# Output projection of a hybrid decoder step: tokens in rows in place of features in rows

## The chip, the cores and the metric

The kernel runs on one core of a Trainium2 chip. The metric is the device time of one execution in microseconds (us), taken as the median over several runs. The engines are TensorE (PE for its matmuls, PEld for its weight loads), VectorE (DVE), ScalarE (ACT), GpSimd (POOL) and SyncE (SP, which here issues the loads of weights). TensorE's clock has two levels, 1.2 and 2.4 GHz; the profile gives the granted clock of a stretch as a share of the full one (0.50 or 1.00 where it does not change within the stretch).

## The reference

One inference step of a decoder with two layers, over 264 tokens: 256 of a prompt and 8 of a sample group, all in float32, with a model width of 1024. Cut to what matters here:

```python
for i in range(DEPTH):                       # DEPTH = 2
    h = rms_norm(x, P['norm_mix_g'][i])
    ...                                      # layer 0: RWKV-7, layer 1: GLA
    mixed = jnp.concatenate([tok, mem_attention(q_mem, mem_k[i], mem_v[i])], axis=-1)
    x = x + mixed @ P['w_out'][i]            # output projection, 1024 x 1024
    x = x + hier_moe(rms_norm(x, P['norm_ffn_g'][i]), P['router_wg'][i], P['router_bg'][i],
                     P['router_we'][i], P['router_be'][i], P['exp_w_up'][i], P['exp_w_down'][i])
```

`hier_moe` takes the logits of 4 groups and 32 experts (36 columns, 40 with padding), picks a group and two experts in it for each token, and runs them as SwiGLU networks with weights of 1024 x 1024 and 512 x 1024 for each of 32 experts.

## The kernel before, in words

The engines' programs are written out by hand, and semaphores join them. Tokens lie in three row blocks, `TILES`: 128 and 128 rows of the prompt and 8 rows of the sample. `x` holds the residual with tokens in rows, `mixedT` the mixers' output with its 1024 features in rows (8 blocks of 128, `KT = 8`) and the 264 tokens as columns. `ps` are the eight PSUM banks.

The output projection of layer l is `output(l)` of TensorE's program. Before the change it makes the result with features in rows. Two halves of `w_out` (512 columns each, `chunk_in()` or `wo1`) give four groups each, so n runs from 0 to 7. Group n is eight matmuls of 128x264 (L775: the weights loaded into the array are a 128x128 block of `w_out`, and `mixedT` moves), then three products by `ident` that add x, turned, into the same bank (L778). ScalarE copies the bank to `oT` (L1314). While the next group runs, `finish(n - 1)` takes `oT` for the router's logits (L759, three products of 40 columns, raw, since the norm's scale comes later) and turns it back to tokens in rows (L763, three transposes). VectorE copies these to x (L1817, L1818) and ScalarE takes their squares (L1561) for the norm. `finish(7)` ends the projection. Behind it stand 41 products of `ident` that nothing reads (`idle_products(WARM[0])`, L749).

VectorE's `route(l)` then adds up the squares (L1654), makes the norm's scale, scales the logits (L1659), and picks the groups and experts until `gates` (L1682). TensorE's next piece, the tokens' ranks in their experts (L1190), waits for `gates`. Then come a few more idle products, the gather of the tokens for the first experts (L1100), and the expert units (L1119), whose weights SyncE loads into a ring of 8 buffers (`load_unit`, L380). A load beyond the ring's eighth waits until TensorE has used a buffer (`m_used`). At the start of `output(l)` TensorE waits for `t_dve` (VectorE's last piece of `mixedT`) and for `router_s` (VectorE has scaled the router's weights `wr` and cleared `ss8`, L1813).

Of the kernel before, what the change touches and what calls it, by code (L numbers as in the profile page):

```python
# [6 lines left out]
ALU = mybir.AluOpType  # L7
# [11 lines left out]
TS = 8  # L19
# [22 lines left out]
EPS = 1e-6  # L42
GN_EPS = 64e-5
# [10 lines left out]
def tiles_through(g):  # L54

    total = 0
    for i, m in enumerate([2, 2] + [w // 128 for _, w in W_IN0[1:]] + [4, 4]):
        total += LORA_TILES.get(i, 0) + m
        if i == g:
            return total  # L60


CHUNKS = 3 + len(W_IN0)
# [91 lines left out]
shift_in shiftT_ps xj lora_s t_dve t_act sum_ps c_ps c_dve c_act c_zero oT_ps o_x dec_out gla_in  # L155
kv1w_in kv1_ps kv1_out kT1_ps kv1_stored vec2_in vec2 k1_in gnorm_in w1_in0 w1_in1 w1_in2 w1_in3 kT1_in p1_ps p1_out
# [4 lines left out]
def build(nc, A, O, dbg=None):  # L161
    with ExitStack() as ctx:
# [199 lines left out]

        oT = [arena[:, AR + 128 + T * n:AR + 128 + T * (n + 1)] for n in range(2)]
# [19 lines left out]
        def _(sp):  # L383
# [66 lines left out]
            def mixer1():  # L450
                sp.dma_start(gng, A["gla_norm_g"][0:1, :].broadcast_to([128, 192])).then_inc(s["gnorm_in"], 16)
                sp.wait_ge(s["kv1_stored"], 48)
                sp.dma_start(kT_1, kT_scr.rearrange("p (a b) -> p a b", a=2)).then_inc(s["kT1_in"], 16)
# [48 lines left out]
            for l in range(DEPTH):  # L502
# [3 lines left out]
                for n in range(UNITS * NQ):  # L506
# [3 lines left out]
                    if n in (6, 7):  # L510
                        sp.wait_ge(s["pj_ps"], tiles_through(n + 2) + 8 * l)
# [104 lines left out]
        def _(pe):  # L616
            sel = lambda b, n: ident[0:TS, b:b + 1].broadcast_to([TS, n])

            def transpose_h(n):
                pe.wait_ge(s["norm_h"], 6 * n - 3)  # L620
                pe.wait_ge(s["pj_out"], tn[0])
# [129 lines left out]
            def output(l):  # L751

                def finish(n):

                    pe.wait_ge(s["pj_out"], tn[0] - (0 if n == KT - 1 else 1))
                    if KT * l + n >= 2:
                        pe.wait_ge(s["o_x"], KT * l + n - 1)
# [9 lines left out]
                n = 0  # L767
                for half in range(2):
                    buf = chunk_in() if l == 0 else wo1[half]
                    if l == 1:  # L770
                        pe.wait_ge(*((s["w1_in0"], 48) if half else (s["w1_in3"], 32)))
                    for b in range(4):
                        p = bank()
                        for i in range(KT):
                            pe.matmul(p[:, 0:T], buf[:, 512 * i + 128 * b:512 * i + 128 * (b + 1)], mixedT[:, i, :], start=(i == 0), stop=False)  # L775

                        for t, (c, m) in enumerate(TILES):
                            last = pe.matmul(p[:, c:c + m], x[0:m, t, 128 * n:128 * (n + 1)], ident[0:m, 0:m], start=False, stop=(t == 2))  # L778
                        tile_done(last)
                        if n > 0:  # L780
                            finish(n - 1)
                        n += 1
                finish(KT - 1)
                idle_products(WARM[0])

# [135 lines left out]
            def mixer1():  # L921
# [33 lines left out]
                pe.wait_ge(s["kT1_in"], 16)  # L955
# [294 lines left out]
        def _(act):  # L1250
# [298 lines left out]
            for l in range(DEPTH):  # L1549
# [7 lines left out]
                def squares(n):  # L1557

                    act.wait_ge(s["o_x"], KT * l + n + 1)
                    for t, (_, m) in enumerate(TILES):  # L1560
                        last = act.activation(h[0:m, t, 128 * n:128 * (n + 1)], x[0:m, t, 128 * n:128 * (n + 1)], ACT.Square, accum_out=ss8[0:m, t, n:n + 1])  # L1561
                    last.then_inc(s["o_sq"], 1)

                for n in range(KT):
                    if n >= 2:
                        act.wait_ge(s["oT_ps"], KT * l + n - 1)
                    out(oT[n % 2], 128)
                    if n == 1:
                        act.wait_ge(s["router_s"], l + 1)
                    if n > 0:  # L1570
                        squares(n - 1)
                squares(KT - 1)
# [41 lines left out]
        def _(dve):  # L1614
# [37 lines left out]
            def route(l):  # L1652
                dve.wait_ge(s["o_sq"], KT * (l + 1))
# [3 lines left out]
                dve.wait_ge(s["logit_ps"], l + 1)  # L1657
# [80 lines left out]
            def setup():  # L1738
# [69 lines left out]
            def output(l):  # L1808
# [5 lines left out]
                for n in range(KT):  # L1814
                    dve.wait_ge(s["oT_ps"], KT * l + n + 1)
                    cols = slice(128 * n, 128 * (n + 1))
                    dve.tensor_copy(x[:, 0:2, cols], ps[2 + n % 2][:, 0:256].rearrange("p (t d) -> p t d", t=2))  # L1817
                    mark(dve.tensor_copy(x[0:TS, 2, cols], ps[2 + n % 2][0:TS, 256:384]), "o_x", KT * l + n + 1)  # L1818
# [178 lines left out]
            def mixer1():  # L1997
# [62 lines left out]
                dve.wait_ge(s["gnorm_in"], 16)  # L2060
# [107 lines left out]
```

## Time and profile before

| what | value |
|---|---|
| median of 3 runs | 1671.73 us (1666.05 to 1673.22) |
| the profiled execution's own time | 1672.15 us |
| its span in the trace | 1670.2 us |
| granted TensorE clock, mean over the span | 0.872 |
| PE busy | 1282.9 us (77%) |
| DVE, ACT, POOL busy | 25%, 15%, 1% of the span |
| read from HBM | 455.12 MB, 277 GB/s over the span |

The busy shares are means over stages with different limits, so none of them says what the stage around the projection is worth. The time outside the span is 1.95 us. The profiled execution is 0.42 us above the median.

### The profile page before, as it was taken

The numbers are of one execution on the slowest core, as the hardware profiler recorded it, in microseconds if no ns is written. First come the engines' busy times: TensorE is split into PE (matmuls) and PEld (weight loads), VectorE is DVE, ScalarE is ACT, GpSimd is POOL, SyncE is SP. The second block draws the span as 40 slices with busy tenths as digits, with TensorE's granted clock in tenths as the row PEclk, the third lists the DMA queues.
The fourth block names the chain that finished last, engine by engine and source line by source line (L and its number), as shares of the span: only waits on it lengthen the run. The fifth ranks groups of instructions, "written<-read, shape, count | busy, mean of one in ns | idle before, by whom it ended". The sixth has DMA issues, their size and how long they took to land.

```text
span 1670.2 us, 21379 instructions
## 1 busy us (share of the span) xinstructions
PE 1282.9 (77%) x9492; PEld 702.9 (42%) x9492; DVE 412.9 (25%) x828; ACT 249.4 (15%) x656; POOL 18.0 (1%) x53
## 2 busy tenths in 40 slices
PE   2968996879977685967665999879977666967754
PEld 1556786877633231513211665548613213312311
DVE  4044567841311011011012132521211011011002
ACT  2110331241201000001001322312201000100100
POOL 1000000000000000000000000000000000000000
PEclk9958899899989778799898887779989987889886
DMA  9410201038499999999997813428599999999993
GB/s 304 148 47 26 76 5 44 18 132 352 161 409 409 409 409 409 408 409 409 409 410 291 268 48 57 163 76 317 236 408 409 408 409 408 409 409 409 409 409 154
DMA packets 147475, 463.65 MB, mean 278 GB/s; under 512 B 12858, under 2 KB 37212, under 8 KB 147180
## 3 DMA queue, kind: packets, MB, share of 16 engines
q1 hardware_dynamic: 145980, 457.78, 71.2%
q0 software_dynamic: 1392, 4.38, 0.8%
q8 instruction: 78, 1.28, 0.3%
q14 instruction: 25, 0.20, 0.0%
HBM read 455.12 MB, written 7.02 MB: 277 GB/s over the span
## 4 chain that ended last, share of the span: by engine, by line
PE 47%; DMA 38%; DVE 7%; SPq 3%; issue 2%; ACT 2%; DVEq 0%; ACTq 0%
DMA slot<-in_exp_w_up 26%; PE bank L1119 8%; PE bank L656 6%; DMA arena<-in_exp_w_up 6%; DMA slot<-in_exp_w_down 6%; PE bank L1100 5%; PE bank L775 4%; PE bank L887 4%; SPq L380 3%; PE bank L940 3%; PE bank L934 3%; PE bank L1130 2%; PE bank L749 1%; PE bank L742 1%; PE bank L675 1%
## 5 line engine op out<-in xcount | busy, mean ns | idle before, releaser
L1119 PE MATMUL bank<-slot,hT 128*32 128x512 f32 x1536 | 232.0, 723 | 133.8 <-DMA slot<-in_exp_w_up 133.8
L1119 PEld LDWEIGHTS bank<-slot,hT 128*32 128x32 f32 x1536 | 49.5, 123 | 301.6 <-DMA slot<-in_exp_w_up 175.9
L1719 DVE SCALAR_TENSOR_TENSOR mixedT<-mixedT,bank 128x512 f32<-128x512 f32 x16 | 11.0, 688 | 509.8 <-ACT mixedT L1275 509.8
L1119 PE MATMUL bank<-slot,mixedT 128*32 128x512 f32 x768 | 100.9, 669 | 37.4 <-DMA slot<-in_exp_w_down 30.6
L1119 PE MATMUL bank<-arena,hT 128*32 128x512 f32 x512 | 80.2, 707 | 40.8 <-DMA arena<-in_exp_w_up 40.8
L1130 PE MATMUL bank<-mixedT,arena 128*128 128x512 f32 (+1 forms) x192 | 90.2, 612 | 12.8 <-ACT mixedT L1284 12.8
L1100 PE MATMUL bank<-arena,h 128*128 128x128 f32 (+1 forms) x384 | 81.8, 351 | 12.1 <-DVE arena L1712 7.8
L1275 ACT ACTIVATE mixedT<-bank 128x512 f32<-128x512 f32 x16 | 9.6, 597 | 532.8 <-PE bank L1119 532.8
L1100 PEld LDWEIGHTS bank<-arena,h 128*128 128x128 f32 (+1 forms) x384 | 62.6, 222 | 37.3 <-issue 12.6
L1731 DVE TENSOR_TENSOR x<-bank,x 128x512 f32<-128x512 f32 (+1 forms) x96 | 66.0, 687 | 36.2 <-PE bank L1130 36.2
L1100 PE MATMUL bank<-gain,h 128*128 128x128 f32 (+1 forms) x384 | 74.8, 329 | 0.0
L775 PE MATMUL bank<-mixedT,slot 128*128 128x264 f32 x256 | 64.3, 407 | 9.7 <-issue 9.7
L1119 PEld LDWEIGHTS bank<-slot,mixedT 128*32 128x32 f32 x768 | 24.0, 119 | 110.6 <-issue 51.1
L1100 PEld LDWEIGHTS bank<-gain,h 128*128 128x128 f32 (+1 forms) x384 | 57.1, 204 | 25.0 <-issue 12.3
L1725 DVE COPY mixedT<-bank 128x512 f32<-128x512 f32 x16 | 11.1, 692 | 225.8 <-PE bank L1119 225.8
L656 PE MATMUL bank<-slot 128*128 128x264 f32 x288 | 64.8, 386 | 0.6 <-ACT arena L1314 0.6
L1130 PEld LDWEIGHTS bank<-mixedT,arena 128*128 128x128 f32 (+1 forms) x192 | 28.4, 161 | 75.9 <-issue 75.9
L1270 ACT ACTIVATE hT<-bank,gainT 128x128 f32<-128x128 f32 x128 | 36.6, 368 | 156.7 <-PE bank L1100 156.7
L656 PEld LDWEIGHTS bank<-slot 128*128 128x128 f32 x288 | 54.6, 190 | 10.3 <-ACT arena L1314 1.0
L775 PEld LDWEIGHTS bank<-mixedT,slot 128*128 128x128 f32 x256 | 50.4, 202 | 18.8 <-DVE arena L1995 8.0
L1119 PEld LDWEIGHTS bank<-arena,hT 128*32 128x32 f32 x512 | 17.5, 120 | 93.4 <-issue 48.7
L1119 PE MATMUL bank<-arena,mixedT 128*32 128x512 f32 x256 | 39.3, 744 | 13.0 <-DMA arena<-in_exp_w_down 6.7
(448 smaller groups left out, 1497.1 us busy)
## 6 DMA issues: line engine op xcount, KB each, us to landing
slot<-in_exp_w_up SPq DMA_DIRECT2D x96, 2048.0 KB, 24.1
slot<-in_exp_w_down SPq DMA_DIRECT2D x48, 2048.0 KB, 24.0
arena<-in_exp_w_up SPq DMA_DIRECT2D x32, 2048.0 KB, 23.6
arena<-in_exp_w_down SPq DMA_DIRECT2D x16, 2048.0 KB, 23.6
slot<-in_w_in SPq DMA_DIRECT2D x6, 1536.0 KB, 7.1
slot<-in_w_out SPq DMA_DIRECT2D x4, 2048.0 KB, 8.6
slot<-in_w_in SPq DMA_DIRECT2D x3, 2048.0 KB, 8.0
slot<-in_w_in SPq DMA_DIRECT2D x5, 1024.0 KB, 5.6
```

The source lines that it names most:

```text
L380: sp.dma_start(ring[buf], src.rearrange("e p n -> p e n")).then_inc(sem, 16)
L656: last = pe.matmul(p[0:m, 0:n], w(k), rhs(k), start=(k == 0), stop=(k == kt - 1))
L675: last = pe.matmul(ps[4 + m][:, :], mem[:, m, 128 * k:128 * (k + 1)], w[:, k, :], start=(k == 0), stop=(k == KT - 1))
L775: pe.matmul(p[:, 0:T], buf[:, 512 * i + 128 * b:512 * i + 128 * (b + 1)], mixedT[:, i, :], start=(i == 0), stop=False)
L887: last = pe.matmul(out, lt(c)[rows, q, :], rh(c)[rows, q, :], start=(i == 0), stop=(i == len(MM[name]) - 1))
L934: last = pe.matmul(p[0:m, 0:T], w(k)[:, c0:c0 + m], rhs(k), start=(k == 0), stop=(k == kt - 1))
L940: last = pe.matmul(p[:, 0:384], hT[:, k, 128 * t:128 * (t + 1)], w[:, k, :], start=(k == 0), stop=(k == KT - 1))
L1100: last = pe.matmul(ps[bank][:, 128 * (k % 4):128 * (k % 4 + 1)], h[0:m, t, 128 * k:128 * (k + 1)], G[par][0:m, t, :], start=(t == 0), stop ...
L1119: last = pe.matmul(ps[bank + half][rows, :], lhs[:, rows], ring[buf][:, e, half * FF:(half + 1) * FF], start=first, stop=last_)
L1130: return pe.matmul(ps[SC_BANK[o]][0:m, :], ST[:, c:c + m], yq[:, FF * n:FF * (n + 1)], start=True, stop=True)
L1270: last = act.activation(xs[par][:, k, :], ps[bank][:, 128 * (k % 4):128 * (k % 4 + 1)], ACT.Copy, scale=gainT[:, KT * l + k:KT * l + k + 1])
L1731: return dve.tensor_tensor(xt, ps[SC_BANK[o]][0:m, :], xt, ALU.add)
```

## The change

The projection is made with tokens in rows. The matmuls of a half now have 128 tokens of `mixedT` as weights, and 512 columns of `w_out` move (`tokens`). The eight sample rows are made by products that have the last 32 columns of `mixedT` as weights, the i-th in column group i % 4 of the array, so that a bank holds four partial sums (`samples`). ScalarE copies that bank to `oS`, and a product with the new constant `pick` adds the four up (`samples_sum`). VectorE adds the banks to x (`add_tokens`, `add_samples`); the three products that added x in TensorE are gone. When x is there, it is turned once, by feature block, for the logits (`transposes`, `logits`), with ScalarE's copy to `oT` between. ScalarE's squares are six of up to 512 columns for a layer in place of 24 of 128. The wait for `router_s` stands ahead of the transposes, no more at the projection's start. `pick` is built by one VectorE operation at the program's start, and two small loads now share a semaphore (`gnorm_in`).

```diff
-                def finish(n):
...
-                    for t, (c, m) in enumerate(TILES):
-                        last = pe.matmul(ps[4 + t][0:m, 0:LG], oT[n % 2][:, c:c + m], wr[:, n, :], start=(n == 0), stop=(n == KT - 1))
...
-                    for t, (c, m) in enumerate(TILES):
-                        last = pe.transpose(ps[2 + n % 2][0:m, 128 * t:128 * (t + 1)], oT[n % 2][:, c:c + m], ident[:, :])
-                    last.then_inc(s["oT_ps"], 1)
+                def tokens(half, t):
+
+                    p = ps[2 * half + t]
+                    for i in range(KT):
+                        last = pe.matmul(p[:, :], mixedT[:, i, 128 * t:128 * (t + 1)], buf[:, i, :], start=(i == 0), stop=(i == KT - 1))
+                    tile_done(last)
+
+                def samples(half):
+
+                    for i in range(KT):
+                        last = pe.matmul(ps[4 + half][32 * (i % 4):32 * (i % 4 + 1), :], mixedT[:, i, T - 32:T], buf[:, i, :], start=(i < 4), stop=(i >= 4))
+                    tile_done(last)
+
+                def samples_sum(half):
+
+                    pe.wait_ge(s["o_sb"], O_STEPS * l + half + 1)
...
+                    pe.matmul(ps[7][0:TS, :], pick[:, :], oS[half], start=True, stop=True).then_inc(s["o_ps"], 1)
+
+                def transposes(n):
+
+                    if n >= 2:
+                        pe.wait_ge(s["o_sb"], O_STEPS * l + n + 1)
+                    for t, (c, m) in enumerate(TILES):
+                        last = pe.transpose(ps[n % 2][:, c:c + m], x[0:m, t, 128 * n:128 * (n + 1)], ident[0:m, 0:m])
+                    last.then_inc(s["o_ps"], 1)
+
+                def logits(n):
+
+                    pe.wait_ge(s["o_sb"], O_STEPS * l + n + 3)
                     for t, (c, m) in enumerate(TILES):
                         last = pe.matmul(ps[4 + t][0:m, 0:LG], oT[n % 2][:, c:c + m], wr[:, n, :], start=(n == 0), stop=(n == KT - 1))
-                    if n == KT - 1:
-                        last.then_inc(s["logit_ps"], 1)
...
-                pe.wait_ge(s["router_s"], l + 1)
...
-                    for b in range(4):
-                        p = bank()
-                        for i in range(KT):
-                            pe.matmul(p[:, 0:T], buf[:, 512 * i + 128 * b:512 * i + 128 * (b + 1)], mixedT[:, i, :], start=(i == 0), stop=False)
...
+                    tokens(half, 0)
+                    if half == 0:
+                        tokens(half, 1)
+                        samples(half)
+                samples(1)
+                samples_sum(0)
+                tokens(1, 1)
+                samples_sum(1)
+                pe.wait_ge(s["router_s"], l + 1)
+                pe.wait_ge(s["o_x"], 6 * l + 4)
+                for n in range(KT):
+                    if n == 4:
+                        pe.wait_ge(s["o_x"], 6 * (l + 1))
+                    transposes(n)
+                    if n > 0:
+                        logits(n - 1)
+                logits(KT - 1)
                 idle_products(WARM[0])
...
+                link(dve.tensor_reduce(pick[:, :], ident[:, :].rearrange("p (j n) -> p n j", j=4)[:, 32 - TS:32, :], AXX, ALU.add))
...
+                def add_tokens(half, t, tile):
...
+                    dve.tensor_tensor(x[:, t, cols], ps[2 * half + t][:, :], x[:, t, cols], ALU.add).then_inc(s["o_x"], 1)
```

On TensorE, this is the start of the projection and the end of its first group before the change (the names behind the arrow are what is read, the first before it what is written):

```order
L775 MATMUL bank<-mixedT,slot 128x264 [waits chunk_in2,pj_out,router_s,t_dve]
L775 MATMUL bank<-mixedT,slot 128x264 x7
L778 MATMUL bank<-ident,x 128x128 x2
L778 MATMUL bank<-ident,x 128x8
L775 MATMUL bank<-mixedT,slot 128x264 [waits pj_out]
```

After the change the same place reads:

```order
L762 MATMUL bank<-slot,mixedT 128x512 [waits chunk_in2,t_dve]
L762 MATMUL bank<-slot,mixedT 128x512 x15
L768 MATMUL bank<-slot,mixedT 32x512 x8
L762 MATMUL bank<-slot,mixedT 128x512 [waits chunk_in0]
L762 MATMUL bank<-slot,mixedT 128x512 x7
```

The 128x264 matmuls with their three adding products have become 128x512 matmuls and 32x512 ones, and the wait for `router_s` has left this place.

Before the change each group's `finish` stands between the wide matmuls of the groups, on TensorE as:

```order
L759 MATMUL bank<-wr,arena 128x40 [waits pj_out]
L759 MATMUL bank<-wr,arena 128x40
L759 MATMUL bank<-wr,arena 8x40
L763 MATMUL bank<-ident,arena 128x128 x2
L763 MATMUL bank<-ident,arena 8x128
```

After the change these rows repeat, eight of them behind all wide matmuls and right ahead of the 41 idle products (a step of the tail):

```order
L783 MATMUL bank<-ident,x 128x128 [waits o_sb]
L783 MATMUL bank<-ident,x 128x128
L783 MATMUL bank<-ident,x 128x8
L790 MATMUL bank<-wr,arena 128x40 [waits o_sb]
L790 MATMUL bank<-wr,arena 128x40
L790 MATMUL bank<-wr,arena 8x40
```

The logits and the transposes have moved from between the wide matmuls to one run without any wide matmul in it, and the transposes now read x, not `oT`.

## Rows read from the trace of the kernel before

**Rows 1.** Windows around both projections: us, busy (x count) of each engine, PEclk, DMA share, GB/s.
```profile
379.10:383.00 3.90, 3.82 (x9) 3.03 (x10) 0.00 (x0) 0.00 (x0) 0.00 (x0) 0.50 0.94 320
383.00:425.30 42.30, 42.30 (x240) 36.16 (x239) 4.27 (x14) 9.04 (x44) 0.00 (x0) 1.00 0.82 322
...
425.30:446.70 21.40, 21.40 (x172) 18.03 (x174) 11.39 (x64) 7.71 (x24) 0.00 (x0) 1.00 0.24 92
446.70:900.00 453.30, 329.04 (x1972) 121.68 (x1968) 51.32 (x77) 31.24 (x87) 0.00 (x0) 0.86 1.02 407
1118.80:1123.70 4.90, 4.83 (x11) 3.83 (x12) 0.00 (x0) 0.00 (x0) 0.00 (x0) 0.50 0.98 329
```

**Rows 2.** Timeline, TensorE's weight loads: start, us, line, operation, xcount [idle before <-releaser].
```profile
379.15 5.32 PEld L775 LDWEIGHTS bank<-mixedT,slot 128*128 128x128 f32 x16 [7.98 <-DVE arena L1995]
...
423.29 0.67 PEld L759 LDWEIGHTS bank<-wr,arena 128*128 128x128 f32 x6
...
424.03 0.26 PEld L763 LDWEIGHTS bank<-ident,arena 128*128 128x128 f32 x3
...
424.31 0.67 PEld L759 LDWEIGHTS bank<-wr,arena 128*128 128x128 f32 x6
...
425.33 9.23 PEld L749 LDWEIGHTS bank<-ident 128*128 128x128 f32 x82
...
1118.84 0.29 PEld L775 LDWEIGHTS bank<-mixedT,slot 128*128 128x128 f32 x1 [1.95 <-DVE arena L2079]
...
1165.52 0.41 PEld L749 LDWEIGHTS bank<-ident 128*128 128x128 f32 x3
```

**Rows 3.** Chain of waits: start, us, engine, line, xcount of a link.
```profile
54.11 13.75 PE bank L675 x32
...
436.56 8.24 PE bank L1100 x48
...
444.81 13.91 PE bank L1119 x128
...
575.95 14.99 PE bank L1100 x48
```

**Rows 4.** Timeline, VectorE ahead of layer 0's projection.
```profile
378.09 0.06 DVE L1995 MEMSET arena<- 128x1 f32 x1
...
379.00 0.08 DVE L1813 MEMSET arena<- 128x24 f32 x1
```

**Rows 5.** Timeline, VectorE's routing and TensorE's wait for it, layer 0.
```profile
430.23 0.58 DVE L1659 SCALAR_TENSOR_TENSOR arena<-bank,arena,br 128x40 f32<-128x40 f32 x3
...
434.59 0.18 PE L1190 MATMUL bank<-arena,before_h 128*128 128x32 bf16 x1
```

**Rows 6.** Windows elsewhere, for the granted clock.
```profile
69.00:73.20 4.20, 4.14 (x26) 2.55 (x24) 0.00 (x0) 3.08 (x8) 2.02 (x3) 1.00 0.38 130
...
371.40:376.20 4.80, 0.00 (x0) 0.00 (x0) 1.23 (x2) 3.37 (x4) 0.00 (x0) 1.00 0.03 6
...
575.95:590.90 14.95, 14.95 (x49) 11.36 (x49) 1.38 (x2) 1.74 (x5) 0.00 (x0) 0.50 1.03 411
...
955.10:959.90 4.80, 3.68 (x23) 2.50 (x22) 0.86 (x2) 4.24 (x11) 0.00 (x0) 1.00 0.76 208
960.00:976.90 16.90, 16.90 (x47) 10.71 (x47) 6.76 (x9) 2.52 (x4) 0.00 (x0) 0.50 0.09 32
...
1112.00:1117.20 5.20, 4.98 (x18) 2.78 (x18) 0.00 (x0) 2.08 (x6) 0.00 (x0) 0.50 0.00 0
```

**Rows 7.** Timeline, three transposes of row blocks (128, 128, 8 rows), twice.
```profile
72.08 0.37 PEld L626 LDWEIGHTS bank<-ident,h 8*128 8x128 f32 x3 [0.17 <-issue]
...
1113.43 0.49 PEld L1092 LDWEIGHTS bank<-ident,slot 8*128 8x128 f32 x3 [0.33 <-issue]
```

**Rows 8.** Page, costliest groups: line, operation, xcount, busy us, mean ns, idle before.
```profile
L1275 ACT ACTIVATE mixedT<-bank 128x512 f32<-128x512 f32 x16 | 9.6, 597 | 532.8 <-PE bank L1119 532.8
...
L1731 DVE TENSOR_TENSOR x<-bank,x 128x512 f32<-128x512 f32 (+1 forms) x96 | 66.0, 687 | 36.2 <-PE bank L1130 36.2
```

More of the change, by code:

```diff
@@ L56, in tiles_through @@
     total = 0
-    for i, m in enumerate([2, 2] + [w // 128 for _, w in W_IN0[1:]] + [4, 4]):
+    for i, m in enumerate([2, 2] + [w // 128 for _, w in W_IN0[1:]] + [3, 3]):
         total += LORA_TILES.get(i, 0) + m
@@ L154 @@
 cache_k cache_v qn_ps qn qb_ps s_score sT_ps s_max s_exp s_prob spT_ps spT sat_ps sat_out
-shift_in shiftT_ps xj lora_s t_dve t_act sum_ps c_ps c_dve c_act c_zero oT_ps o_x dec_out gla_in
-kv1w_in kv1_ps kv1_out kT1_ps kv1_stored vec2_in vec2 k1_in gnorm_in w1_in0 w1_in1 w1_in2 w1_in3 kT1_in p1_ps p1_out
+shift_in shiftT_ps xj lora_s t_dve t_act sum_ps c_ps c_dve c_act c_zero o_ps o_sb o_x dec_out gla_in
+kv1w_in kv1_ps kv1_out kT1_ps kv1_stored vec2_in vec2 k1_in gnorm_in w1_in0 w1_in1 w1_in2 w1_in3 p1_ps p1_out
 g_abs g_log g_dec g_sub g_exp g_mul kh_ps kh_out ga_ps ga_out gd_ps gz go_ps go_out gsq gs_a gs_vps gs_add gs_q gs_ps gs_out g_tanh g_silu gm_ps
@@ L361, in build @@
         assert b_.at <= 12288, b_.at
+        oS = [arena[:, 3400 + 512 * n:3400 + 512 * (n + 1)] for n in range(2)]
+        pick = sb("pick", TS)
         oT = [arena[:, AR + 128 + T * n:AR + 128 + T * (n + 1)] for n in range(2)]
@@ L767, in output @@
-                n = 0
+                    last.then_inc(s["logit_ps"], 1)
                 for half in range(2):
-                    buf = chunk_in() if l == 0 else wo1[half]
+                    buf = k3((chunk_in() if l == 0 else wo1[half])[:, 0:KT * 512], KT)
                     if l == 1:
                         pe.wait_ge(*((s["w1_in0"], 48) if half else (s["w1_in3"], 32)))
-                    for b in range(4):
-                        p = bank()
-                        for i in range(KT):
-                            pe.matmul(p[:, 0:T], buf[:, 512 * i + 128 * b:512 * i + 128 * (b + 1)], mixedT[:, i, :], start=(i == 0), stop=False)
-                        for t, (c, m) in enumerate(TILES):
[L778 to L782, printed above, removed]
@@ L1555, in _, with squares, copy_samples @@
                     mixer1()
[L1557 to L1562, printed above, removed]
+                def squares(half, t, at):
+                    m = TILES[t][1]
+                    act.wait_ge(s["o_x"], 6 * l + at)
+                    cols = slice(512 * half, 512 * (half + 1))
+                    act.activation(h[0:m, t, cols], x[0:m, t, cols], ACT.Square, accum_out=ss8[0:m, t, half:half + 1]).then_inc(s["o_sq"], 1)
+                def copy_samples(half):
+                    act.wait_ge(s["pj_ps"], tn[0] + 6 * l + (3, 5)[half])
+                    act.copy(oS[half], ps[4 + half][:, :]).then_inc(s["o_sb"], 1)
+                copy_samples(0)
+                act.wait_ge(s["router_s"], l + 1)
+                squares(0, 0, 1)
+                squares(0, 1, 2)
+                copy_samples(1)
+                squares(1, 0, 3)
+                squares(0, 2, 4)
                 for n in range(KT):
+                    act.wait_ge(s["o_ps"], O_STEPS * l + n + 3)
                     if n >= 2:
[L1566 to L1572, printed above, removed]
+                        act.wait_ge(s["logit_ps"], KT * l + n - 1)
+                    act.copy(oT[n % 2], ps[n % 2][:, 0:T]).then_inc(s["o_sb"], 1)
+                    if n < 2:
+                        squares(1, n + 1, 5 + n)
                 act.wait_ge(s["rs"], l + 1)
@@ L1813, in output, with add_samples @@
                 dve.memset(ss8, 0.0).then_inc(s["router_s"], 1)
[L1814 to L1818, printed above, removed]
+                def add_tokens(half, t, tile):
+                    cols = slice(512 * half, 512 * (half + 1))
+                    dve.wait_ge(s["pj_ps"], PROJECTED + 6 * l + tile)
+                    dve.tensor_tensor(x[:, t, cols], ps[2 * half + t][:, :], x[:, t, cols], ALU.add).then_inc(s["o_x"], 1)
+                def add_samples(half):
+                    cols = slice(512 * half, 512 * (half + 1))
+                    dve.wait_ge(s["o_ps"], O_STEPS * l + half + 1)
+                    dve.tensor_tensor(x[0:TS, 2, cols], ps[7][0:TS, :], x[0:TS, 2, cols], ALU.add).then_inc(s["o_x"], 1)
+                add_tokens(0, 0, 1)
+                add_tokens(0, 1, 2)
+                add_tokens(1, 0, 4)
+                add_samples(0)
+                add_tokens(1, 1, 6)
+                add_samples(1)
+                dve.wait_ge(s["o_x"], 6 * (l + 1))
                 mark(dve.memset(sq[:, 0:1], 0.0), "x_out", l + 1)
```

22 lines of the change are left out of this document (11 added, 11 removed).

## The prediction

> **What bounds the kernel now.** I read the windows around the projections first. From 446.7 us the DMA engines are full (share 1.02, 407 GB/s), and they stay so to 900; ahead of that, from 425.3 to 446.7, they are nearly idle (0.24) while TensorE is busy for all of 21.40 us [rows 1]. The ring's eight buffers are loaded by then, and the next load waits for the first expert unit to release one. So the experts' stream of weights sets the end, and TensorE's run from the start of the projection to the first released buffer sets when that stream begins. A microsecond taken from this run moves the stream and the end by a microsecond; this holds once for each layer.
>
> Second, the timeline of TensorE. In layer 0 the projection begins at 379.15 and its last group hands over to the idle products at 425.33, which is 46.18 us; in layer 1 it is 1118.84 to 1165.52, 46.68 us; together 92.86 [rows 2]. TensorE is busy in all of it but 0.1 us [rows 1], so there is no stall to win, only work. The clock is at 0.50 (1.2 GHz) for the first 3.9 us of layer 0's projection and the first 4.9 us of layer 1's [rows 1]: what is done there takes twice as long.
>
> Third, what stands behind: TensorE's ranks (L1190) begin at 434.59, right behind the idle products, which take about 9.3 us from 425.33 [rows 2, 5]. VectorE's routing, which they also wait for, runs from 430.23 until then, 4.36 us from the scaled logits to the gates [rows 5].
>
> **The new work at full clock, a layer.** Token tiles: 32 matmuls of 128x512. The nearest row is 16 such matmuls (32 records, two for each float32 matmul) in 13.75 us, 0.859 each [rows 3], so 27.50. Samples: 16 products of 32x512 in four column groups, shaped like the experts' first products, 64 of which take 13.91 us (128 records) [rows 3], 0.217 each, so 3.48. Two sums of the partials are 512-column products without company: 1.72. Then the tail, eight steps of three transposes and three 40-column products. Transposes of row blocks cost 0.37 and a gap of 0.17 [rows 7]; logits 0.74, from 423.29 to 424.03 [rows 2]; a step is 1.28 and the tail 10.24. The sum is 27.50 + 3.48 + 1.72 + 10.24 = 42.94, for both layers 85.88.
>
> **The start.** TensorE no longer waits for `router_s` there, so it follows the VectorE memset that ends at 378.15, not the one that ends at 379.08 [rows 4]: 0.93 us earlier in layer 0; I take 0.95 for each layer, 1.9 together. The slow stretch stays. If the clock rises at the same moments as before, it is 4.85 and 5.85 us long and half of it is lost: 2.4 + 2.9 = 5.3 us. (If it rises as long after the start as before, 4.4.)
>
> **Hidden parts.** VectorE's adds of 0.69 us [rows 8] lie beside matmuls: the tail's first transpose needs the half 0 columns, added while tile (1, 1) runs for 6.9 us, and step 4 needs the last adds, some 1.5 us of work, behind 5.1 us of tail. Were they late, the price is those 1.5 us. ScalarE's 512-column squares (0.60 [rows 8], with their accumulators perhaps 0.8) stand between the copies to `oT`; a step of 1.28 covers a copy and two steps a square, and without that cover two squares would cost 1 to 1.5 us a layer. The squares are done before the logits, so the norm's scale leaves the path behind them; but the gates would then be ready 4.4 us after the logits while the idle products take 9.3, so this earns nothing, and hides up to 4.9 us of delay on VectorE. `pick` adds one small reduction to VectorE's start: its nearest is a product of 128x40 in 0.19 (three in 0.58 [rows 5]), so +0.2 us at most, and below nothing isn't possible. The merged semaphore waits for two loads issued one behind the other: 0.
>
> With the clock at full in the tail the change is worth 92.86 − (85.88 + 5.3 − 1.9) = 3.6 us, less 0.2: 3.4. This is 1668.8 against the profiled execution's 1672.15, which lies 0.42 above the median, and 1668.3 on the median's scale, on which all that follows stands.
>
> **The clock in the tail.** Before, thin work stood between wide matmuls, and the clock stayed at 1.00 from 383.0 to 446.7 [rows 1]. Now 10 us hold nothing but transposes and 40-column products. The trace has such stretches. At 69.0 to 73.2 TensorE ran 24 transposes, 4.14 us busy, at 1.00 [rows 6]. From 955.1 to 959.9, 4.80 us of mainly transposes and thin products (3.68 busy), were granted 1.00, and 960.0 begins a stretch at 0.50 [rows 6]; likewise 371.4 to 376.2, idle, ahead of the slow start at 379.1 [rows 1, 6]. So rows of thin work stand on both sides, one that kept the clock and two (one without any work) that ended in a fall; the tail is twice as long as any of them.
>
> The Trainium skill ("TensorE: Matmul & The Clock Gate", Part 4: PE-mode transpose) says the full clock doesn't engage for transpose mode, which "doesn't count as PE-busy the same way". That speaks against this change; the 4.2 us of transposes at 1.00 disagree over that length, the fall at 960 agrees. By the page alone the whole tail would be slow, the slower rival below.
>
> The price: I place the fall as far into the tail as the two stretches that ended in one are long, 4.8 us; 5.44 us are left, 4.25 steps. At 0.50 three transposes take 0.49 + 0.33 = 0.82 in place of 0.54 [rows 6, 7]. For the logits the bounds are 0.74 (all overhead) and 1.48 (all clock); the transposes' ratio is 1.52, that of the gather 14.99/8.24 = 1.82 [rows 3, 6]; between them I take 1.24, nearer the gather, which is matmuls too. A step is then 2.06, 0.78 more; 4.25 steps give 3.3. The idle products then begin slow and need, as at the starts, 3.9 to 4.9 us to raise the clock [rows 1], half of which is lost: 2.2. So 5.5 a layer, 11.0 for both: 11.0 − 3.4 = 7.6 above before, **1679.3**.
>
> Ends: with the fall 2.2 us in (half of the transposes' 4.2 us) it is 6.3 steps, +7.1 a layer, 1682.5; 7.5 us in, 2.1 steps, +3.9, 1676.1; logits at 1.48 add up to 1.0 a layer, 1.02 for 0.78 a step. The own range of this case is 1675 to 1684.
>
> **Rivals.**
> *The clock holds in the tail* (1668.3). For it: the transposes at 69.0 to 73.2. Against it: the fall at 960 and the tail's length.
> *It falls in one layer only*, half of the 11.0: 1673.8. For it: the two layers' clocks do not rise equally long after the start [rows 1].
> *The clock falls at the tail's very start* in both layers: eight steps, 6.2, and 2.2 are +8.4 a layer, 16.8 − 3.4 = 13.4 above before, 1685.1. It decides the sign of my test once the loss is over 5.9 us a layer (8.4 + 3.4, halved). Against it: 4.2 us of transposes at full clock.
> *Faster than before:* the clock holds and the tail is cheaper than priced, since transposes behind other work took 0.28 (424.03 to 424.31) and logits 0.67 [rows 2], a step of 0.95: 16 × 0.33 = 5.3 less, 1663.0. It passes 0.5% from 0.31 a step on. Against it: the 0.28 are transposes that read a full-height `oT`; the gap of 0.17 stood where row blocks of 8 were turned [rows 7], as here.
> That the projection isn't the path can't be: the DMA engines wait for it [rows 1].
>
> **How the numbers follow.** A measurement of this kernel can tell about 0.5%, 8.4 us, from no change; so faster is below 1663.4 and slower above 1680.1. Chances: the fall part way into the tail in both layers 0.55, the clock holds 0.22, one layer 0.08, the early fall 0.08, the cheap tail 0.07. The first case's own range reaches from 1675 to 1684, with somewhat under half of it above 1680.1, say 0.24 of the 0.55; with the early fall, slower is 0.32. Faster is the cheap tail, 0.07. The rest, 0.61, is the same. The range takes in all but the cheap tail: from 1666.5, which is the held clock less the 0.9 for an earlier rise at the start and less half a microsecond of execution spread (0.42, the profiled one above the median), rounded, to the early fall with the layers' rounding, 1685.5.
>
> **What would show it.** Right: eight steps of the tail on TensorE behind the sum of the samples, steps of about 1.3 us and then of about 2.1, a granted clock of 0.50 in the end of the tail and the start of the idle products in both layers; token tiles of 6.9 us, samples of 1.7; TensorE's gather at 1.00; L1190 begins behind idle products with the gates ready before. Wrong: a clock of 1.00 through the tail, TensorE's sample products at 0.8 us each (no company in the column groups, 16 × 0.64 = 10 us a layer more), waits for `o_sb` or `o_x` between the steps, or a stream that begins at a time other than the first released buffer.

## The result, and the profile after

The changed kernel takes 1674.27 us (1670.86 to 1676.86, 13 runs) against 1667.63 us of the kernel before (1663.66 to 1674.63, 13 runs). The ratio is 1.0034 with an interval of 1.002 to 1.0049: 5.7 us slower, between 3.3 and 8.2. The forecast was 7.6 us above the kernel before.

The first view is TensorE's timeline of layer 0 in the changed kernel, which answers to [rows 2]: start, duration, line, operation, count of records.

```profile
377.51 15.95 PE L762 MATMUL bank<-slot,mixedT 128*128 128x512 f32 x32 [6.84 <-DVE arena L2050]
393.39 1.93 PE L768 MATMUL bank<-slot,mixedT 128*32 128x512 f32 x16
395.25 7.13 PE L762 MATMUL bank<-slot,mixedT 128*128 128x512 f32 x16
402.31 1.92 PE L768 MATMUL bank<-slot,mixedT 128*32 128x512 f32 x16
404.05 1.02 PE L776 MATMUL bank<-arena,pick 128*8 128x512 f32 x2
...
413.02 1.11 PE L783 MATMUL bank<-ident,x 128*128 128x128 f32 x6
414.09 0.81 PE L790 MATMUL bank<-wr,arena 128*128 128x40 f32 x6
...
417.87 0.81 PE L790 MATMUL bank<-wr,arena 128*128 128x40 f32 x6
418.61 0.63 PE L783 MATMUL bank<-ident,x 128*128 128x128 f32 x3
419.17 1.31 PE L790 MATMUL bank<-wr,arena 128*128 128x40 f32 x6
420.41 0.89 PE L783 MATMUL bank<-ident,x 128*128 128x128 f32 x3
...
423.29 2.55 PE L790 MATMUL bank<-wr,arena 128*128 128x40 f32 x12
425.77 11.07 PE L754 MATMUL bank<-ident 128*128 128x128 f32 x82
436.68 0.18 PE L1220 MATMUL bank<-arena,before_h 128*128 128x32 bf16 x1
```

The wide work of the changed kernel ends at 413.02, 12.3 us before the old projection's end at 425.33 [rows 2]. The tail spends this: the same logits take 0.74 us up to the step at 417.87 and 1.24 from 419.17 on (start to start), the transposes 0.53 and then 0.82. The tail ends at 425.77, and the 41 idle products take 10.9 us more, where they took 9.3 [rows 2, 5]. The ranks (L1220) start 2.1 us later than before in layer 0 [rows 5], although the projection began 1.64 us earlier.

The windows of the same kernel show why. They answer to [rows 1]; the number before the last two of each line is the granted clock.

```profile
377.50:381.40 3.90, 3.89 (x5) 1.81 (x6) 0.73 (x3) 0.00 (x0) 0.00 (x0) 0.50 0.69 229
...
413.00:418.90 5.90, 5.90 (x42) 4.34 (x41) 3.04 (x16) 2.94 (x9) 0.00 (x0) 1.00 1.02 409
418.90:425.80 6.90, 6.90 (x34) 5.27 (x32) 0.00 (x0) 3.16 (x6) 0.00 (x0) 0.51 0.18 71
...
1156.20:1159.80 3.60, 3.60 (x26) 2.59 (x25) 1.59 (x7) 2.18 (x7) 0.00 (x0) 0.99 0.99 361
1159.80:1170.50 10.70, 10.70 (x50) 8.04 (x49) 1.45 (x9) 3.90 (x8) 0.00 (x0) 0.50 0.29 114
1170.50:1173.90 3.40, 3.40 (x19) 3.40 (x19) 3.02 (x25) 1.11 (x2) 0.00 (x0) 0.58 0.00 0
```

TensorE is busy in every microsecond of the tail, so no wait for ScalarE's copies is at work. The clock falls from 1.00 to 0.50 inside the tail, 5.9 us into it in layer 0 and 3.6 us in layer 1, and the idle products behind it begin at the low level (0.58 over the last window). In the changed kernel VectorE has the gates long before TensorE reads them:

```profile
429.96 0.26 DVE L1722 TENSOR_TENSOR arena<-arena 128x96 bf16<-128x96 f32 x1
```

That operation ends at 430.22, and the ranks that wait for it start at 436.68: 6.46 us of idle products stand between. In the kernel before, the same operation ends at 434.50, and the ranks start at 434.59 [rows 5]:

```profile
434.24 0.26 DVE L1682 TENSOR_TENSOR arena<-arena 128x96 bf16<-128x96 f32 x1
```

SyncE's first load that waits for a released buffer shows what the end of the kernel sees of all this. In the kernel before it stands at 446.7 [rows 1] and, in layer 1, with the program's last matmuls below it, so:

```profile
1186.91 3.80 SPq L380 DMA_DIRECT2D slot<-in_exp_w_down  x3
...
1643.51 3.64 PE L1119 MATMUL bank<-slot,mixedT 128*32 128x512 f32 x16 [1.89 <-DMA slot<-in_exp_w_down]
1647.94 7.89 PE L1130 MATMUL bank<-mixedT,arena 128*128 128x512 f32 x12 [0.80 <-ACT mixedT L1284]
```

In the changed kernel:

```profile
448.81 3.80 SPq L385 DMA_DIRECT2D slot<-in_exp_w_down  x3
...
1193.23 3.80 SPq L385 DMA_DIRECT2D slot<-in_exp_w_down  x3
...
1649.98 1.92 PE L1149 MATMUL bank<-slot,mixedT 128*32 128x512 f32 x16 [1.69 <-DMA slot<-in_exp_w_down]
1652.70 5.48 PE L1160 MATMUL bank<-mixedT,arena 128*128 128x512 f32 x12 [0.80 <-ACT mixedT L1314]
```

The stream of layer 1 starts 6.3 us later and its last load lands 6.5 us later (the last unit starts at 1649.98, not 1643.51). The two profiled executions differ by 2.3 us only, since the last two pieces behind the stream took 1.92 and 5.48 us in one and 3.64 and 7.89 in the other: the granted clock over the last unit is 1.00 in the changed kernel's execution and 0.50 in the other's. These 4.1 us don't belong to the change: from the landing of the last load to the end of the span it is 26.7 us in the kernel before and 22.5 in the changed one, but 26.7 again in e9_weave_no_fill, which has the new projection too. A single execution scatters by that much, so below the length of the path is compared beside the ratios of many runs.

### The profile page after: what moved, and what is told of

It is laid out like the page before. It is cut to its first block, busy times and chain, and to the rows that moved or that the text cites. A ratio compares the mean times of both kernels' runs of the same rounds, so it can differ in the third digit from the quotient of the medians.

```text
span 1672.5 us, 20962 instructions
## 1 busy us (share of the span) xinstructions
PE 1306.3 (78%) x9340; PEld 679.6 (41%) x9340; DVE 411.4 (25%) x809; ACT 242.5 (15%) x588; POOL 18.0 (1%) x53
## 4 chain that ended last, share of the span: by engine, by line
PE 49%; DMA 36%; DVE 7%; SPq 3%; issue 3%; ACT 2%; DVEq 0%; ACTq 0%
DMA slot<-in_exp_w_up 25%; PE bank L1149 9%; PE bank L661 6%; DMA arena<-in_exp_w_up 6%; DMA slot<-in_exp_w_down 6%; PE bank L1130 5%; PE bank L762 4%; PE bank L917 4%; PE bank L970 3%; PE bank L964 3%; SPq L385 3%; PE bank L1160 2%; PE bank L754 1%; PE bank L790 1%; PE bank L747 1%
## 5 line engine op out<-in xcount | busy, mean ns | idle before, releaser
L1149 PE MATMUL bank<-slot,hT 128*32 128x512 f32 x1536 | 242.0, 752 | 127.9 <-DMA slot<-in_exp_w_up 127.8
L1149 PE MATMUL bank<-arena,hT 128*32 128x512 f32 x512 | 84.6, 737 | 34.7 <-DMA arena<-in_exp_w_up 34.7
L1130 PE MATMUL bank<-arena,h 128*128 128x128 f32 (+1 forms) x384 | 88.2, 371 | 15.5 <-DVE arena L1752 15.5
L1130 PEld LDWEIGHTS bank<-arena,h 128*128 128x128 f32 (+1 forms) x384 | 67.4, 238 | 43.0 <-DVE arena L1752 17.3
L1130 PE MATMUL bank<-gain,h 128*128 128x128 f32 (+1 forms) x384 | 68.4, 309 | 0.0
L762 PE MATMUL bank<-slot,mixedT 128*128 128x512 f32 x128 | 61.4, 638 | 7.8 <-DVE arena L2050 6.8
L1130 PEld LDWEIGHTS bank<-gain,h 128*128 128x128 f32 (+1 forms) x384 | 52.5, 189 | 23.4 <-issue 9.0
L970 PE MATMUL bank<-slot,hT 128*128 128x384 f32 x128 | 47.5, 532 | 0.0
```

The lines of the kernel that those rows point to most:

```text
L762: last = pe.matmul(p[:, :], mixedT[:, i, 128 * t:128 * (t + 1)], buf[:, i, :], start=(i == 0), stop=(i == KT - 1))
L970: last = pe.matmul(p[:, 0:384], hT[:, k, 128 * t:128 * (t + 1)], w[:, k, :], start=(k == 0), stop=(k == KT - 1))
L1130: last = pe.matmul(ps[bank][:, 128 * (k % 4):128 * (k % 4 + 1)], h[0:m, t, 128 * k:128 * (k + 1)], G[par][0:m, t, :], start=(t == 0), stop ...
L1149: last = pe.matmul(ps[bank + half][rows, :], lhs[:, rows], ring[buf][:, e, half * FF:(half + 1) * FF], start=first, stop=last_)
```

## The experiments

For each kernel the table gives the path: from the end of VectorE's small memset ahead of the projection, which the changed projection follows within 0.05 us, to the first product of the ranks, layer 0 plus layer 1, from the timelines. The ratio is that of runs against the kernel before on the same chip.

| kernel | path, us | against before | ratio (95% interval) |
|---|---|---|---|
| before | 56.44 + 56.94 = 113.38 | | 1 |
| changed | 59.22 + 61.42 = 120.64 | +7.26 | 1.0034 (1.002 to 1.0049) |
| e1_idle22 | 54.97 + 57.17 = 112.14 | −1.24 | 0.9999 (0.9982 to 1.0015) |
| e2_spread | 55.67 + 56.07 = 111.74 | −1.64 | 0.9995 (0.9975 to 1.0015) |
| e3_turn_by_matmul | 65.72 + 66.74 = 132.46 | +19.08 | 1.0077 (1.0057 to 1.0098) |
| e4_samples_twice | 63.09 + 64.87 = 127.96 | +14.58 | 1.0068 (1.0047 to 1.0089) |
| e5_weave | 52.57 + 53.60 = 106.17 | −7.21 | 0.9939 (0.9927 to 0.9952) |
| e6_before_idle31 | 56.40 + 56.90 = 113.30 | −0.08 | 1.0006 (0.9992 to 1.002) |
| e7_before_start | 55.98 + 56.50 = 112.48 | −0.90 | 1.0000 (0.9987 to 1.0014) |
| e8_spread_idle19 | 54.10 + 54.98 = 109.08 | −4.30 | 0.9992 (0.9981 to 1.0004) |
| e9_weave_no_fill | 53.70 + 53.26 = 106.96 | −6.42 | 0.9955 (0.9938 to 0.9973) |
| e10_spread1 | 55.17 + 56.19 = 111.36 | −2.02 | 0.9988 (0.9976 to 1.0) |
| e11_weave_fill1 | 52.18 + 52.58 = 104.76 | −8.62 | 0.9960 (0.9945 to 0.9975) |
| e12_turn_fill1 | 58.23 + 59.34 = 117.57 | +4.19 | one run, 1671.39 us |

Behind the path nearly everything is as long in one kernel as in another. From the first product of the ranks to SyncE's first load that waits for a released buffer it is 12.13 or 12.14 us in all fourteen profiles and both layers, but for one (layer 1 of e6_before_idle31, below); from that load to the landing of the layer's last one it is 456.4 to 457.6 us. So the stream of weights hides nothing of the path. The ratios follow the paths only roughly all the same: e3_turn_by_matmul is 12.9 us slower (9.5 to 16.3) for a path longer by 19.1, e8_spread_idle19 1.3 us faster (−0.7 to 3.2) for 4.3, and e5_weave 10.2 us faster (8.0 to 12.2) for 7.2. A path is that of one execution, and all that lies outside it adds up to between 1550.6 and 1558.4 us from one profile to the next. Why these three miss by more than their intervals stays open.

**Is it the clock?** The same 41 idle products, 16 of them moved into the tail (`FILL = 2`):

```diff
                     transposes(n)
                     if n > 0:
                         logits(n - 1)
+                    for _ in range(FILL):
+                        pe.matmul(ps[2][:, 0:128], ident[:, :], ident[:, :], start=True, stop=True)
                 logits(KT - 1)
-                idle_products(WARM[0])
+                idle_products(WARM[0] - FILL * KT)
```

> The changed kernel with the same 41 idle products, two of them after each of the tail's eight steps and 25 behind it. Theory (the clock falls because the tail holds thin work alone): the granted clock stays at 1.00 from the token tiles to the gather, steps are 1.26 + 0.45 = 1.71 us throughout, logits 0.74 in all of them, and the first released buffer comes 4.1 us earlier in layer 0 and 5.6 us in layer 1 than in the changed kernel; 9.7 in all, ratio about 0.9975. Rival (a step's length comes from the round trip over ScalarE's copy, and products put into it only fill a wait): no wide change of the steps, ratio 1.003. Rival (the clock falls from the tail however it is filled that lightly): steps grow to 2.06 + 0.9, ratio 1.003 to 1.006.

The windows over both tails of this kernel:

```profile
415.70:429.60 13.90, 13.90 (x105) 11.48 (x104) 3.04 (x16) 5.67 (x14) 0.00 (x0) 1.00 0.49 194
1152.50:1166.50 14.00, 14.00 (x105) 11.51 (x104) 3.04 (x16) 5.68 (x14) 0.00 (x0) 1.00 0.48 189
```

The clock stays at 1.00, steps are 1.75 us throughout with logits of 0.74, and the path is 8.9 us shorter than the changed kernel's with the same work in it: 9.7 were expected. The rival of a round trip over ScalarE falls: in a step that waits for a copy, products put in would fill the wait, but the steps grew by 0.49 us (from 1.26) for the 0.55 us of products put in. The ratio's interval doesn't exclude 0.9975, nor no difference to the kernel before, but it lies below the changed kernel's.

**One product a step** in place of two:

> The changed kernel with one idle product in each of the tail's steps (33 behind it), where e2_spread had two. If the theory is right that it is the share of wide work in the tail that decides, one product a step is the middle: either it holds (1.00 through the tail, from start to ranks 55.6 us as with two, ratio 0.9995) or the clock falls, later than in the changed kernel or as late, and the path is between 55.6 and 59.2 us in layer 0, ratio 1.001 to 1.003.

```profile
413.10:425.30 12.20, 12.20 (x89) 9.72 (x88) 3.05 (x16) 5.34 (x14) 0.00 (x0) 1.00 0.61 243
1148.00:1161.50 13.50, 13.50 (x92) 9.81 (x90) 3.74 (x17) 5.30 (x14) 0.00 (x0) 1.00 0.59 229
```

The clock stays at 1.00 in both layers, with 24 transposes in each tail, and the path is 55.2 us in layer 0 (55.6 expected).

**Is it the transposes?** The turning made by ordinary products, first in the changed kernel's order, then with one idle product a step:

```diff
-last = pe.transpose(ps[n % 2][:, c:c + m], x[0:m, t, 128 * n:128 * (n + 1)], ident[0:m, 0:m])
+last = pe.matmul(ps[n % 2][:, c:c + m], x[0:m, t, 128 * n:128 * (n + 1)], ident[0:m, 0:m], start=True, stop=True)
```

> The changed kernel with its 24 transposes a layer made as ordinary float32 products by the identity, everything else as it was. If it is the transposes that let the clock fall: the clock stays at 1.00 in the tail, a step costs perhaps 0.1 to 0.3 us more (1.4 to 1.55), and the 9.7 us come back less 1.6 to 4.8, ratio 0.998 to 1.0005. If the 40-column products alone are thin enough: the clock still falls 3 to 7 us into the tail, every step is longer by its slower turning, and the ratio is 1.005 to 1.008.

```profile
415.10:420.90 5.80, 5.80 (x41) 4.98 (x40) 2.97 (x16) 2.70 (x8) 0.00 (x0) 1.00 1.02 408
421.30:434.00 12.70, 12.70 (x54) 10.70 (x54) 0.00 (x0) 3.47 (x6) 0.00 (x0) 0.50 0.07 26
1161.70:1168.40 6.70, 6.70 (x48) 5.66 (x47) 3.04 (x16) 2.70 (x8) 0.00 (x0) 1.00 0.95 367
1168.80:1179.80 11.00, 11.00 (x48) 9.30 (x48) 0.00 (x0) 3.39 (x6) 0.00 (x0) 0.50 0.01 3
```

> The changed kernel with the turning made by ordinary products (as e3_turn_by_matmul) and one idle product in each step (as e10_spread1). If wide work of any kind keeps the clock and e3_turn_by_matmul was only a little short of it: 1.00 through the tail in both layers, steps of 1.93 us. If ordinary products in place of transposes are what lets it fall: 0.50 from some 4 to 7 us into the tail.

```profile
414.00:429.20 15.20, 15.20 (x113) 13.18 (x112) 3.04 (x16) 5.39 (x14) 0.00 (x0) 1.00 0.50 199
1153.60:1168.80 15.20, 15.20 (x113) 13.17 (x112) 3.04 (x16) 5.42 (x14) 0.00 (x0) 1.00 0.44 166
```

Without a single transpose the clock fell 6 to 7 us into the tail all the same, and with one more product in each step it stayed at 1.00. So the fall doesn't need transposes, and transposes don't force it: in these profiles, one of each kernel, the tails of either kind fell without the added product and held with it. Which part of a step lets the clock fall was not separated further; the 24 products of 40 columns are in every tail. The turning by ordinary products was dearer than the 0.1 to 0.3 us a step expected (steps of 1.70 us at full clock and 2.91 at half, against 1.26 and 2.06); the ratio, 1.0077, is among those expected for a fall (1.005 to 1.008).

**Does each microsecond count?** The sample products made twice:

```diff
-                    for i in range(KT):
+                    for i in [*range(KT), *range(KT)]:
```

> The changed kernel with the products of the sample rows made twice (the first pass's sums are overwritten by, or added to, the second's; the time alone is of interest). Theory (each microsecond of TensorE's work in the projection moves the end by one): 16 more products of 0.22 us a half, +1.8 us a half, +3.5 a layer, +7 in all, ratio 1.0076. Rival (the projection is partly hidden, as by loads of weights that are late anyway): under +2, ratio below 1.005.

```profile
406.84 3.64 PE L768 MATMUL bank<-slot,mixedT 128*32 128x512 f32 x32
```

These are the 16 products of half 1 in layer 0, 3.64 us in place of 1.92. The path is 7.3 us longer than the changed kernel's, as expected, and the ratio is 1.0068, 0.0034 (5.7 us) above it. With both intervals that is an estimated 1.4 to 10 us: the added work reaches the end, but the ratios alone don't tell whether all of it does.

**The slack in front of the gates.** The changed kernel with `WARM = (22, 5)`, then the kernel before with `WARM = (31, 5)`, then the spread tail with `idle_products(19)` behind it:

> The changed kernel with 22 idle products behind each projection in place of 41. Theory (TensorE's run up to the first released buffer sets the end, and the gates are ready some 4.4 us after the last logits, well ahead of the idle products' end at 10.9 us): the 19 products left out, 0.227 us each, come off the path in both layers, 4.3 us a layer, 8.6 in all, so from 1.0034 of the kernel before to about 0.998; the wait for the gates stays at 0 and the gather (L1130) stays at 8.4 us. Rival (the idle products also hold the clock up for the gather): the clock is at 0.50 when the gather begins, which then takes 15 us in place of 8.4, so about +2.3 a layer, ratio 1.006. Rival (the gates are late): TensorE waits for them as long as before, ratio 1.0034.

> The kernel before with 31 idle products in place of 41. Theory (before the change the routing ends together with the idle products, at 434.5, because the norm's scale comes after the last logits): TensorE waits for the gates for some 2.2 us in place of running products, the ranks begin at the same moment, ratio 1.000. Rival (the idle products alone held the ranks): 2.27 us a layer earlier, ratio 0.9973. If the clock falls in the wait, the gather takes 15 us in place of 8.2: ratio 1.008.

> The changed kernel with two idle products in each of the tail's steps and 19 behind it in place of 25. Theory (the gates come 4.4 us after the last logits, 19 products fill 4.3): 1.3 us a layer earlier than with 25, no wait for the gates over 0.3 us, the clock at 1.00 throughout; 2.6 us in all, ratio 0.998. Rival (the wait for the gates takes the place of the products): as with 25, 0.9995.

In the changed kernel the 19 products are pure waste: the path is 8.5 us shorter (8.6 expected), the gather keeps 8.41 us, and the ranks still start 2.2 and 1.9 us behind the gates. The ratio, 0.9999, is 0.0035 (5.8 us) below the changed kernel's; the 0.998 expected lies just outside its interval. In the kernel before, ten fewer leave the ranks where they were, since TensorE then waits; the first rank product in layer 0 of e6_before_idle31 reads

```profile
435.42 0.19 PE L1190 MATMUL bank<-arena,before_h 128*128 128x32 bf16 x1 [2.02 <-DVE arena L1682]
```

with 2.02 us of wait for the gates. That wait isn't always free. In layer 1 of the same run the clock was at 0.50 behind it, and the few idle products ahead of the gather took 2.50 us in place of 1.38:

```profile
1176.26 2.50 PE L749 MATMUL bank<-ident 128*128 128x128 f32 x10
1178.56 8.74 PE L1100 MATMUL bank<-arena,h 128*128 128x128 f32 x48
```

From the ranks to the first released buffer it was 13.60 us there, 1.47 more than elsewhere, which the path in the table does not show. In layer 0 the clock held.

So the early squares did take the norm off the routing (the gates come 4.4 us after the last step in the changed kernel, 9.2 in the kernel before), and this is worth nothing until idle products are taken out. With both, in the spread tail of e8_spread_idle19, the ranks start 0.06 us behind the gates, and the path is 2.7 us shorter than with 25 products; the ratio (0.9992; the 0.998 expected lies just outside its interval) doesn't separate the two.

**The start alone**, in the kernel before:

```diff
                 def finish(n):

+                    if n == 0:
+                        pe.wait_ge(s["router_s"], l + 1)
...
-                pe.wait_ge(s["router_s"], l + 1)
                 n = 0
```

> The kernel before with its wait for the router's weights (router_s) moved from the projection's start to the first logits: this part of the change alone. Theory: both projections start 0.95 us earlier and every later stage with them, 1.9 in all, ratio 0.9989. Rival (the start only moves the moment of the clock's rise, or the next wait takes its place): no gain, 1.000.

The projection follows the memset by 0.05 us in place of 1.0, but the path is shorter by 0.46 and 0.44 us only. The part of the projection at 0.50 is 4.9 and 5.9 us long, where it was 3.9 and 4.9 [rows 1]: the time won at the start is spent at half clock, and about half of it is lost. 0.9 us are below what the ratio can show.

**A version from these parts.** The sample products of both halves ahead of tile (1, 0), their sums among its matmuls, steps 0 to 3 between pairs of matmuls of tile (1, 1), steps 4 to 7 with idle products, 20 products behind (`WARM = (20, 5)`). VectorE's adds and ScalarE's squares are put in the matching order; cut to TensorE's part:

```diff
                 samples(1)
+                tokens(1, 0, 0, 2)
                 samples_sum(0)
-                tokens(1, 1)
+                tokens(1, 0, 2, 5)
                 samples_sum(1)
+                tokens(1, 0, 5, 8)
...
                     if n == 4:
+                        logits(3)
                         pe.wait_ge(s["o_x"], 6 * (l + 1))
                     transposes(n)
-                    if n > 0:
+                    if n > 0 and n != 4:
                         logits(n - 1)
+                    if n < 4:
+                        tokens(1, 1, 2 * n, 2 * n + 2)
+                    else:
+                        for _ in range(FILL):
+                            pe.matmul(ps[2][:, 0:128], ident[:, :], ident[:, :], start=True, stop=True)
```

with `FILL` 2, 0 and 1:

> The changed kernel in another order: both halves' sample products and their sums ahead of or among tile (1, 0), steps 0 to 3 of the tail between pairs of tile (1, 1)'s matmuls, steps 4 to 7 behind it with two idle products each, and 20 idle products at the end in place of 41. Theory (the new form of the projection is shorter work, the loss lies in the clock, and the idle products in excess of the routing's 4.4 us are waste): the clock stays at 1.00, and from the start of the projection to the ranks it is 1.9 + 33.6 + 8 x 1.26 + 1.8 + 4.5 = 51.9 us in layer 0 against 55.4 in the kernel before; with the earlier start some 4.4 us a layer, ratio about 0.9947. Rival (half of the tail without wide matmuls is still enough for the clock to fall): 0.50 in the last steps, 2 to 4 us a layer back, 0.998 to 1.000. Rival (the adds by VectorE are late for step 4): a wait of 1 us for o_x in each layer, 0.996.

> The woven order of e5_weave without the eight idle products in steps 4 to 7, whose thin run is then 5.1 us long. If the clock holds over it: 1.8 us a layer less than e5_weave, 3.6 in all, ratio about 0.992. If it falls there (in the changed kernel it fell 6.1 us into the tail in layer 0 and 3.6 us in layer 1): at least layer 1 loses, one or two steps of 0.8 us and idle products that begin at 0.50 (1.5 to 2 us): between 0 and 2 us of the 3.6 are left, ratio 0.993 to 0.995, with 0.50 shown in the end of the tail.

> The woven order with one idle product in steps 4 to 7 in place of two. As e10_spread1 kept 1.00 with one product in every step and e9_weave_no_fill fell without any, the clock should hold: 0.9 us a layer less than e5_weave, 1.8 in all, ratio 0.993 by the path (0.9928 from e5_weave's 0.9939), the gather at 8.4 us. If the clock falls in the last steps: 0.995 to 0.996 as e9_weave_no_fill.

With two products a step the path is 7.2 us shorter than the kernel before's (4.4 a layer expected, 3.9 and 3.3 came) and the ratio 0.9939 (0.9947 expected): faster than both kernels, as forecast. Step 4 does wait 0.24 us for VectorE's add:

```profile
420.90 0.59 PE L785 MATMUL bank<-ident,x 128*128 128x128 f32 x3 [0.24 <-DVE x L1876]
```

With none, the thin run of some 5 us ends in a fall in both layers; layer 1 shows it so:

```profile
1156.50:1161.50 5.00, 5.00 (x36) 3.77 (x36) 2.34 (x15) 2.54 (x7) 0.00 (x0) 0.98 0.94 332
1161.60:1164.50 2.90, 2.90 (x14) 2.90 (x14) 2.52 (x20) 2.61 (x3) 0.00 (x0) 0.50 0.33 134
```

and what the eight products left out a layer should save (3.6 us expected if the clock held) goes to slow idle products: the path is 0.8 us longer than with two. With one the clock holds and the path is the shortest, 1.4 us below that with two (1.8 expected), yet the ratio is 0.9960 against 0.9939, and the 0.9928 expected lies outside its interval. The two intervals overlap; which of the two is faster stays open.

## Why the prediction was right or wrong

The clock fell in the tail as forecast, and the time rose. The step of the prediction that failed is the one from the sum to the answer: "A measurement of this kernel can tell about 0.5%, 8.4 us, from no change". No row stood behind it; known were three runs of the kernel before, 7.2 us apart. On it a forecast of +7.6 us, 0.45%, went under "the same" with a chance of 0.61, and slower got 0.32. Thirteen runs of each kernel told 0.15%, and the +0.34% measured (0.20 to 0.49) stands clear of no change: slower. A forecast of 0.45% should have been read as slower.

In the sum itself three terms had the wrong size. The wide work was put at 65.4 us and took 67.5, the slow start at 5.3 and took 4.5, the slow idle products at 4.4 and took 3.0. That they leave the sum within 0.2 us of the measured path is luck, since the errors cancel.

The terms of the sum, both layers, against the changed kernel's timeline:

| term | forecast | measured |
|---|---|---|
| wide work at full clock | 65.4 | 67.5 (tiles 7.06, samples 1.74 to 1.86, sums 0.95) |
| the tail at full clock | 20.5 | 20.2 (steps of 1.26) |
| slow start, lost | 5.3 | 4.5 (15.88 and 16.82 for tiles of 14.12) |
| earlier start | −1.9 | −1.9 |
| the fall in the tail | 6.6 | 6.8 (2.6 and 4.2) |
| slow idle products | 4.4 | 3.0 (10.9 and 10.6 against 9.3) |
| path against before (92.9, start to idle products) | +7.4 | +7.3 |

- **The bound**, TensorE's run up to the first released buffer, stood: e4_samples_twice lengthened it by 7.3 us and the time with it, e2_spread and e1_idle22 shortened it, and the stream behind it was 456.4 to 457.6 us long in every profile. That a microsecond of it is a microsecond of time is not shown as exactly: three of the ratios in the table miss their paths by more than their intervals.
- **The prices** were good to a few hundredths where a row had the same shape: transposes at half clock were forecast at 0.82 and took 0.82, at full clock 0.54 and 0.53. Logits at half clock were forecast at 1.24 and took 1.24, but that was a choice between 0.74 and 1.48, so some luck is in it. The token tiles were taken from a row of 0.859 us a matmul and took 0.883; samples and sums were a little dearer too; together 2.1 us more.
- **The start**: the part at 0.50 was put at 4.85 and 5.85 us. In layer 0 the clock rose as long after the start as before, 3.9 us (window 377.50 to 381.40), which the prediction had named as the other case; in layer 1 the slow part was 5.9 us.
- **The fall** came in both layers, part way. It was placed at 4.8 us and came at 5.9 and 3.6, which nearly cancels: luck again. The rivals that the clock holds, that it falls in one layer only or at the tail's start, and that the tail is cheap (transposes took 0.53 us and logits 0.74, not 0.28 and 0.67) are out. e2_spread shows the cause by moving work alone. The Trainium skill ("TensorE: Matmul & The Clock Gate", Part 4: PE-mode transpose) was cited against the change with its sentence that the full clock doesn't engage for transpose mode, and the tail did lose its clock. Transpose mode doesn't explain it here: e3_turn_by_matmul fell without transposes, e10_spread1 kept 1.00 over 12.2 us with 24 of them among its steps, and transposes took 0.53 us at 1.00 where they took 0.82 at 0.50.
- **The idle products** hid the gain of the early squares, as forecast, 6.5 and 6.2 us of slack in place of 4.9, for they ran slowly themselves.
- **The clock-held case** was forecast at −3.4 us. e2_spread's path is −1.6: the difference is about the 2.1 us by which the wide work was too cheap in the sum.
- **The absolute time**, 1679.3, was on the scale of three runs of the kernel before with a median of 1671.73; thirteen gave 1667.63, 4.1 us less. The ratio is free of it. The 0.2 us put down for `pick` can't be read: the memset ahead of layer 0's projection ends between 377.5 and 381.2 us in the fourteen profiles.

That the measured 5.7 us are less than the path's 7.3 lies within the interval; no other cause was looked for.

## What to carry to other kernels

Where work stands can matter as much as how long it takes: collecting the thin products of a loop behind its wide ones made the wide work shorter, but the clock fell in the thin run. Before a stage is shortened, look at what waits at its end; here idle products sized for the old routing took the routing's gain. Idle products among the thin steps, and the surplus behind them taken out, brought the change level with the kernel before (0.9992 in e8_spread_idle19); it paid when half of the thin steps also went between wide matmuls (0.9939 to 0.9960). And an effect half as large as the spread of single executions (5.7 us against 11 us in the kernel before) still shows in a dozen runs.

## What the runs showed of the hardware

A tail of eight thin steps in which TensorE was busy all the time lost the full clock all the same, 3.6 to 6.9 us into it, with transposes in it (changed kernel) and without (e3_turn_by_matmul). With one product of 128x128 more in each step it kept 1.00 (e10_spread1, e12_turn_fill1). Forty-one products that only hold the clock cost 9.3 us at full clock, but 10.9 and 10.6 when the clock had fallen ahead of them, since they then begin at half clock. An earlier start into a slow stretch returned half of itself (0.46 and 0.44 of 0.95 us). And a wait of 2.02 us ahead of the ranks left the clock at 1.00 in one layer and was followed by 0.50 in the other (e6_before_idle31). At the end of the stream, which is bound by DMA, the same last two pieces took 7.4 us in one execution (1.92 + 5.48) and 11.5 in another (3.64 + 7.89), with the clock of the last unit at 1.00 and at 0.50.
